# First-mixer phases of six runs instead of seven, with heads' pairs 0 and 3, 1 and 2 together

## The chip, the cores and the metric

The kernel runs on one core of a Trainium2 chip. The metric is device time in microseconds (us) of one execution; lower is better.

## The reference

Two layers over 1024 tokens of width 1024, all in float32. Of each layer only what surrounds the change matters here:

```python
h = rms_norm(x, g_mix)
qa, ka, va, qb, kb, vb, gate_logits = split(h @ w_in)
y_a = chunk_band_relbias_attention(qa, ka, va, rel_table) @ w_branch_a   # mixer A
y_b = sliding_window_sink_gqa(rope(qb), rope(kb), vb, sinks) @ w_branch_b  # mixer B
g_a, g_b = split(sigmoid(gate_logits + b_gate))
x = x + (g_a * y_a + g_b * y_b) @ w_out
x = x + (silu(g_part) * u_part) @ w_down      # of rms_norm(x) @ w_gate_up
```

Mixer A has 8 heads of 64. A 64-token chunk sees itself and the 8 chunks before it (576 keys) with a bias by relative distance. Mixer B has 8 query heads and 2 key heads, with rotary positions, a window of two chunks and a sink per head.

## The kernel before

Features lie on the 128 partitions, tokens on the free axis. The attention of a layer is 128 units in 4 groups of 32. The first 16 units of a group are its phase of mixer A: 8 blocks of 128 queries ("pairs" p = 0 to 7, for each of two heads e = 0, 1; unit u is e = u % 2 of pair u % 16 // 2). The last 16 are its phase of mixer B. Pair p of mixer A has min(p + 1, 5) blocks of 128 keys, so 128, 256, 384, 512 and then 640 columns of scores.

Units are taken in runs. `run_start` and `run_end` give a run's first and last unit. Before, a phase A has seven runs: pairs 0 and 1 together, then pairs 2 to 7 alone. A phase B has two runs of 8 units. Every engine walks a loop over the unit number s, written by hand, and all ordering between engines is by semaphores.

TensorE (PE), at the start of a run: `scores` of this run; `weigh` (probabilities times values) of the run two before; `turn_run`, the 128x128 transposes of the probabilities of the run before, into PSUM banks 5 and 1 (`t_ps`) and, where a pair has five blocks, the fifth block of both heads into half of bank 7 (`last_ps`); sometimes `turn_inverse`, one transpose of eight units' 1/sum; sometimes `turn_values`, which transposes 512 tokens of values into bank 7; and then the fill: `fill_rate(s)` steps of the product of h with the gate weights (`gate_step`, lines L1395, L1399 and L1400, three 128x512 matmuls a step). Eight steps make one half tile of gate logits in bank 0, which VectorE takes away in `scale_logit` before the next half tile may open there:

```python
if k == 0: ...
    pe.wait_ge(logit_ready, L * GATE_HALVES + i)      # gate_step, first step of half tile i
```

`FILL_A` and `FILL_B` say how many steps each run has. Before, each half tile of gates ends with the last step of some run.

VectorE (DVE), unit by unit: `row_max` (bias, row minimum of the negated scores, PSUM to the buffer of probabilities; it waits until the scores of its whole run are made), at the second unit of a run `take_inverse` and `take_heads` (outputs from PSUM to `x_sb`), reciprocals, `scale_logit` at the end of a run, and three rotary operations for each 512 columns of q of mixer B: `turn_half` at units c and c + 1 and `add_half` at c + 2, where c is 4 and 9 of a phase A of groups 1 to 3. `scores` of a run waits until `row_max` has read all of the run before (`scores_free`).

ScalarE (ACT): at the first unit of a run `soften` (exp) of that unit, then `take_turned` (transposed probabilities from PSUM to `probs_t`: two copies of up to 512 columns and one of 256 for fifth blocks) and `take_values`; then `soften` of the run's other units.

There are four buffers of probabilities. Outputs of mixer A lie in bank 6, those of mixer B in banks 4 and 6 in turn. GpSimd (POOL) splits gate weights and scales finished heads by 1/sum, SyncE (SP) issues the loads and stores, those of 1/sum through DRAM too.

Of the kernel before, what the change touches and what calls it, by code (L numbers as in the profile page):

```python
# [33 lines left out]
P = 128  # L34
# [175 lines left out]

def unit(u):

    g, r = divmod(u, UNITS_PER_GROUP)
    return "AB"[r // PHASE], g, r % 2, r % PHASE // 2


def run_start(u):
    return u & (~7 if unit(u)[0] == "B" else ~3 if u % PHASE < 4 else ~1)


def run_end(u):
    return u | (7 if unit(u)[0] == "B" else 3 if u % PHASE < 4 else 1)


FILL_A = ((8, 0, 4, 4, 2, 2, 2, 2),) + ((2, 0, 3, 2, 1, 1, 1, 0),) * (GROUPS - 1)
# [79 lines left out]
def quarters_at(s, afters):  # L305
    return [2 * eight + j for j, after in enumerate(afters) for eight in inverses_at(s, after)]
# [20 lines left out]
def turned_through(u):  # L327

    runs = {run_start(v): 3 if wide(v) else 2 for v in range(u + 1)}
    return sum(runs.values())  # L330
# [6 lines left out]
def last_wide(u):  # L337
    return max((v for v in range(u + 1) if wide(v)), default=None)
# [10 lines left out]
B_EIGHTS = EIGHTS // 2  # L349
SAVED_AFTER, SPREAD_AFTER, SCALED_AFTER = 3, (5, 6), (7, 9)  # L350
# [107 lines left out]
def build(nc, x_t, w_lin, w_gu, w_dn_a, w_dn_b, gains, gate_bias, rel, sink_in, rope_in, consts_in, out_t):  # L458
    ctx = ExitStack()
    with ctx:  # L460
# [127 lines left out]
        def s_ps(u, cols):  # L588
# [4 lines left out]
            if p == 1:  # L593
                return bank(2 + e)[:, P:P + cols]
            if cols <= HALF:
                return bank(2 + e)[:, 0:cols]
# [71 lines left out]
        def scale(engine, L, quarter):  # L668
# [5 lines left out]
            if mixer == "A":  # L674
                x = x_sb[:, g, p * P:(p + 2) * P]
                return engine.tensor_tensor(x, x, rows[:, :], ALU.mult)
# [4 lines left out]
        def turned_to(u):  # L681
            if unit(u)[0] == "A":
                return probs_t[:, u % 2, P if u % PHASE in (2, 3) else 0:]
            return probs_t[:, u % EIGHT // 4, u % 4 * P:(u % 4 + 1) * P]
# [7 lines left out]
        def soft(u):  # L692

            r = u % PHASE
            if unit(u)[0] == "B":
                first = (r // 4 + r // EIGHT) * P
                return probs[(r + 2) % NPROBS][:, first:first + P]
            if r < 4:
                return probs[r % 2][:, r // 2 * P:3 * P]
            return probs[(r + 2) % NPROBS][:, :]  # L700

        def soft_last(u):

            first = u // PHASE * PHASE
            if unit(u)[0] == "B":
                return first - NPROBS + u % NPROBS
            return first - EIGHT - 1 if u - first < 6 else u - NPROBS
# [681 lines left out]
        def _(pe):  # L1389
# [131 lines left out]
            def scores(L, u):  # L1521
# [3 lines left out]
                if mixer == "A":  # L1525
                    if u % PHASE in (0, PHASE // 2):
                        pe.wait_ge(keys_loaded[p // 4], 32 * (L * GROUPS + g + 1))
                    _, cols = score_columns("A", g, p)
                    k0 = (p + 1) * P - cols
                    if u % PHASE == 0:  # L1530
                        for pair in range(2):
                            for e in range(2):
                                rows = slice(e * HD, (e + 1) * HD)
                                width = (pair + 1) * P
                                pe.matmul(s_ps(u + 2 * pair + e, width), qa[g % 2][rows, pair * P:(pair + 1) * P], ka[g % 2][rows, 0:width],
                                          start=True, stop=True).then_inc(scores_done, 1)
                        return
                    pieces = ((0, 0, cols), (1, 0, cols)) if cols <= HALF else ((0, HALF, cols), (1, P, cols), (0, 0, HALF), (1, 0, P))
                    for n, (e, c, d) in enumerate(pieces):
# [3 lines left out]
                        mm = pe.matmul(s_ps(u + e, cols)[:, c:d], qa[g % 2][rows, p * P:(p + 1) * P], ka[g % 2][rows, k0 + c:k0 + d],  # L1543
                                       start=True, stop=True)
                        if n != 1 or cols <= HALF:
# [12 lines left out]
            def turn_run(L, last):  # L1558
# [18 lines left out]
                for e in range(2):  # L1577
                    for u in range(first + e, last + 1, 2):
                        at_col = P if u - first > 1 else 0
                        pe.wait_ge(softened, softened_through(L, u))  # L1580
                        for j in range(min(key_blocks(mixer, unit(u)[3]), A_BLOCKS - 1)):
                            mm = pe.transpose(t_ps[e][:, at_col + j * P:at_col + (j + 1) * P], soft(u)[:, j * P:(j + 1) * P], ident[:, :])  # L1582
                    mm.then_inc(turned, 1)
                if wide(last):
                    pe.wait_ge(v_ready, L * VALUES + values_before(last + 1))
                    for u in (first, last):
                        mm = pe.transpose(last_ps[:, (u - first) * P:(u - first + 1) * P], soft(u)[:, HALF:A_COLS], ident[:, :])
                    mm.then_inc(turned, 1)

            def weigh(L, u):  # L1590
# [17 lines left out]
                taken = L * HEAD_PAIRS + (u // 2 - (1 if p == 1 else 0) if mixer == "A" else run_start(u) // 2 - (2 if p % 4 < 2 else 0))  # L1608
# [1788 lines left out]
```

## Time and profile before

| | |
|---|---|
| median of 3 runs | 2589.5 us (2589.29 to 2591.73) |
| profiled execution, its own time | 2588.69 us |
| span of its profile | 2586.9 us |
| TensorE busy | 2557.4 us, 99% |
| VectorE, ScalarE, GpSimd busy | 1823.0, 1038.8, 286.4 us |

The profile was taken of one execution. Its own time is 1.8 us over the span of its instructions and 0.8 us under the median of the three runs. A matmul's end is modelled, so its row reads longer than the distance to the next matmul's start; the distances between starts say how fast TensorE moves. The matmuls on float32 heads (scores, weighing, transposes) show two rows each, those of the fills one.

### The profile page before, as it was taken

The page shows a single profiled execution, that of the slowest core. Times are in us where ns is not written, and L with a number is a line of the kernel's source. Part 1 is how long each engine was busy: PE and PEld are TensorE (multiplying, and loading weights), DVE is VectorE, ACT ScalarE, POOL GpSimd, SP SyncE. Part 2 cuts the span into 40 slices and gives each one's busy share as a digit, 9 for nine tenths or more (in the row PEclk, how much of TensorE's full clock was granted, in tenths as well). Part 3 has the DMA queues.
Part 4 walks back from the last instruction along what each step waited for, and adds up shares of the span by engine and source line. Part 5 has one row for each costly group of instructions (what it writes and reads, how often), then busy time and mean ns, then how long its engine had stood idle before and what let it go on. Part 6 is the DMA issues. An engine that isn't in the chain of part 4 may idle for free. (4 is left out here: it accounts for less than half of the span.)

```text
span 2586.9 us, 35453 instructions
## 1 busy us (share of the span) xinstructions
PE 2557.4 (99%) x12822; PEld 2095.1 (81%) x12822; DVE 1823.0 (70%) x3321; ACT 1038.8 (40%) x2035; POOL 286.4 (11%) x442
## 2 busy tenths in 40 slices
PE   8999999999999999999999999999999999999998
PEld 6888777888888888888778887778888888888886
DVE  8766555644888777768996665555459777776687
ACT  6222466522533333344542225664235333333444
POOL 0000232344000000000000002224430000000000
PEclk9999999999999999999999999999999999999999
DMA  4323543453133233395423345425422233225843
GB/s 149 130 102 114 176 140 118 135 178 115 60 116 109 90 107 122 99 280 162 151 102 117 111 136 160 145 84 179 151 106 92 88 106 118 91 97 169 260 117 126
DMA packets 200332, 336.92 MB, mean 130 GB/s; under 512 B 18672, under 2 KB 79968, under 8 KB 200160
## 3 DMA queue, kind: packets, MB, share of 16 engines
q1 hardware_dynamic: 191936, 311.47, 36.5%
q10 hardware_dynamic: 8224, 23.20, 2.6%
q8 instruction: 103, 1.69, 0.3%
q14 instruction: 69, 0.57, 0.1%
HBM read 240.76 MB, written 92.92 MB: 129 GB/s over the span
## 5 line engine op out<-in xcount | busy, mean ns | idle before, releaser
L1407 PE MATMUL ps<-op_hi,up_hi 128*128 128x512 f32 x1232 | 479.9, 389 | 2.5 <-DVE third_sum L2996 2.5
L1409 PE MATMUL ps<-op_hi,up_lo 128*128 128x512 f32 x1232 | 479.3, 389 | 0.0
L1408 PE MATMUL ps<-op_lo,up_hi 128*128 128x512 f32 x1232 | 479.3, 389 | 0.0
L1407 PE MATMUL ps<-in_hi,up_hi 128*128 128x512 f32 x728 | 285.0, 392 | 2.6 <-DVE up_lo L2491 2.1
L1408 PE MATMUL ps<-in_lo,up_hi 128*128 128x512 f32 x728 | 283.7, 390 | 0.0
L1409 PE MATMUL ps<-in_hi,up_lo 128*128 128x512 f32 x728 | 283.7, 390 | 0.0
L1407 PEld LDWEIGHTS ps<-op_hi,up_hi 128*128 128x128 f32 x1232 | 231.3, 188 | 51.0 <-issue 3.3
L1409 PEld LDWEIGHTS ps<-op_hi,up_lo 128*128 128x128 f32 x1232 | 231.3, 188 | 48.2
L1408 PEld LDWEIGHTS ps<-op_lo,up_hi 128*128 128x128 f32 x1232 | 231.3, 188 | 47.8
L2091 ACT ACTIVATE up_hi<-up_raw 128x512 fp32r<-128x512 f32 x252 | 158.1, 630 | 278.5 <-PE ps L1409 271.6
L1360 POOL CAST w_hi<-w_raw 128x256 fp32r<-128x256 f32 x184 | 81.5, 485 | 1468.0 <-DMA w_raw<-w_lin 1209.9
L1407 PE MATMUL ps<-act_hi,dn_hi 128*128 128x512 f32 x616 | 240.5, 390 | 1.2 <-DVE dn_lo L3171 1.2
L1408 PE MATMUL ps<-act_lo,dn_hi 128*128 128x512 f32 x616 | 239.7, 389 | 0.0
L1409 PE MATMUL ps<-act_hi,dn_lo 128*128 128x512 f32 x616 | 239.7, 389 | 0.0
L1944 ACT ACTIVATE probs<-probs,neg_max 128x128 f32<-128x128 f32 (+5 forms) x256 | 138.5, 545 | 145.8 <-DVE neg_max L2788 144.9
L1841 ACT ACTIVATE up_hi<-w_quarter 128x512 fp32r<-128x512 f32 x156 | 96.7, 628 | 193.8 <-PE ps L1409 182.8
L2963 DVE TENSOR_TENSOR up_lo<-up_raw,up_hi 128x512 fp32r<-128x512 f32 x252 | 172.7, 687 | 0.0
L2118 ACT ACTIVATE act_hi<-act_raw 128x512 fp32r<-128x512 f32 x154 | 97.0, 630 | 176.7 <-DMA act_raw<-ff_saved 173.5
L3169 DVE TENSOR_TENSOR act_lo<-act_raw,act_hi 128x512 fp32r<-128x512 f32 x154 | 106.3, 690 | 82.6 <-ACT act_hi L2118 81.8
L1407 PEld LDWEIGHTS ps<-in_hi,up_hi 128*128 128x128 f32 x728 | 137.0, 188 | 32.0 <-DVE up_lo L2491 3.3
L1365 POOL TENSOR_TENSOR w_lo<-w_raw,w_hi 128x256 fp32r<-128x256 f32 x192 | 160.6, 866 | 0.0
L1409 PEld LDWEIGHTS ps<-in_hi,up_lo 128*128 128x128 f32 x728 | 136.9, 188 | 28.4
(255 smaller groups left out, 4758.1 us busy)
## 6 DMA issues: line engine op xcount, KB each, us to landing
up_raw<-w_gu SPq DMA_DIRECT2D x42, 1024.0 KB, 5.1
act_raw<-ff_saved SPq DMA_DIRECT2D x154, 256.0 KB, 2.8
w_quarter<-w_lin SPq DMA_DIRECT2D x52, 512.0 KB, 4.5
w_raw<-w_lin SPq DMA_DIRECT2D x48, 512.0 KB, 4.2
ff_saved<-ff_block SPq DMA_DIRECT2D x88, 256.0 KB, 2.0
ff_saved<-ff_mix SPq DMA_DIRECT2D x66, 256.0 KB, 2.0
gated<-gates_saved SPq DMA_DIRECT2D x32, 512.0 KB, 4.2
dn<-w_dn_a SPq DMA_DIRECT2D x48, 256.0 KB, 4.0
```

Source lines behind the costliest of these rows:

```text
L1360: pool.tensor_copy(w_hi[slot][:, k, :], w_raw[raw][:, k, :]).then_inc(hi_made, 1)
L1365: op = pool.tensor_tensor(w_lo[slot][:, k, :], w_raw[raw][:, k, :], w_hi[slot][:, k, :], ALU.subtract)
L1407: pe.matmul(out, w1, x1, start=first, stop=False, skip_group_check=True)
L1408: pe.matmul(out, w1, x0, start=False, stop=False, skip_group_check=True)
L1409: return pe.matmul(out, w0, x1, start=False, stop=last, skip_group_check=True)
L1841: act.activation(up_hi[s % PRODUCTS][:, :, :], in_weight(q, i), ACT.Copy).then_inc(in_raised, 1)
L1944: act.activation(buf[:, c0:c1], buf[:, c0:c1], ACT.Exp, bias=neg_max[:, stat_of(u)], scale=-1.0, accum_out=row_sum[:, stat_of(u)]).then_in ...
L2091: act.activation(up_hi[s % PRODUCTS][:, :, :], up_src(q, i), ACT.Copy).then_inc(up_raised, 1)
L2118: act.activation(act_hi[r][:, :], act_raw[r][:, :], ACT.Copy).then_inc(act_raised, 1)
L2963: dve.tensor_tensor(up_lo[s % PRODUCTS][:, :, :], up_src(q, i), up_hi[s % PRODUCTS][:, :, :], ALU.subtract).then_inc(up_split, 1)
L3169: dve.tensor_tensor(act_lo[r][:, :], act_raw[r][:, :], act_hi[r][:, :], ALU.subtract)
```

## The change

It changes the order of mixer A's pairs to 0, 3, 1, 2, 4, 5, 6, 7 (`A_ORDER`), and the phase becomes six runs: pairs 0 and 3, pairs 1 and 2, and pairs 4 to 7 alone. The two runs of four units have five blocks for each head, like a single pair of 640 columns. All runs of mixer A now put their last block of keys into `last_ps`, and wait as those of five blocks did. The fills of a phase A become (8, 6, 4, 2, 2, 2) steps in the first group (before 8, 4, 4, 2, 2, 2, 2), and (3, 3, 1, 1, 1, 1) in the others (before 2, 3, 2, 1, 1, 1, 0). All outputs of a run lie in bank 6, of mixer B too except in the last phase, and VectorE waits for all outputs of a run before it copies the first. The transposes of 1/sum are moved (`INVERSE_LATER`). The four buffers of probabilities become two sets, taken by runs in turn, so that `row_max` waits for the transposes of the run two before. In the last phase the scaling of probabilities is two operations of 512 columns instead of four of 256.

```diff
+A_ORDER = (0, 3, 1, 2, 4, 5, 6, 7)
 def unit(u):
     g, r = divmod(u, UNITS_PER_GROUP)
-    return "AB"[r // PHASE], g, r % 2, r % PHASE // 2
+    p = r % PHASE // 2
+    return ("A", g, r % 2, A_ORDER[p]) if r < PHASE else ("B", g, r % 2, p)
 def run_start(u):
-    return u & (~7 if unit(u)[0] == "B" else ~3 if u % PHASE < 4 else ~1)
+    return u & (~7 if unit(u)[0] == "B" else ~3 if u % PHASE < PHASE // 2 else ~1)
...
-FILL_A = ((8, 0, 4, 4, 2, 2, 2, 2),) + ((2, 0, 3, 2, 1, 1, 1, 0),) * (GROUPS - 1)
+FILL_A = ((8, 0, 6, 0, 4, 2, 2, 2),) + ((3, 0, 3, 0, 1, 1, 1, 1),) * (GROUPS - 1)
...
 def inverse_at(eight):
     weighed = weighed_at(EIGHT * eight + EIGHT - 1)
-    return weighed + (4 if weighed % UNITS_PER_GROUP == 2 else 0)
+    return weighed if weighed == HELD else weighed + INVERSE_LATER[eight % len(INVERSE_LATER)]
...
-def last_wide(u):
-    return max((v for v in range(u + 1) if wide(v)), default=None)
+def last_full(u):
+    return max((v for v in range(u + 1) if unit(v)[0] == "A"), default=None)
+def block_place(p):
+    return A_BLOCKS - 1 - p if p < 2 else 0
+INVERSE_LATER = (2, 0, 8, 6)
...
         def o_ps(u):
-            mixer, _, _, p = unit(u)
-            if mixer == "A":
-                return bank(6)[:, P if p == 1 else 0:2 * P if p == 1 else P]
+            if u < LAST_UNIT - EIGHT:
+                place = (u - run_start(u)) // 2
+                return bank(6)[:, place * P:(place + 1) * P]
...
         def soft_last(u):
...
+            return run_start(run_start(u) - 1) - 1 if run_start(u) > 0 else -1
...
             def turn_values(L, s, c):
-                if last_wide(run_start(s) - 1) is not None:
-                    pe.wait_ge(turned_ready, L * TURNS + turned_through(last_wide(run_start(s) - 1)))
+                if last_full(run_start(s) - 1) is not None:
+                    pe.wait_ge(turned_ready, L * TURNS + turned_through(last_full(run_start(s) - 1)))
...
             def scores(L, u):
-                    if u % PHASE == 0:
-                        for pair in range(2):
-                            for e in range(2):
+                    if u % PHASE < EIGHT:
+                        for n, (other, e) in enumerate(((0, 0), (2, 1), (2, 0), (0, 1))):
...
             def turn_run(L, last):
-                if wide(last):
-                    pe.wait_ge(v_ready, L * VALUES + values_before(last + 1))
-                    for u in (first, last):
+                pe.wait_ge(v_ready, L * VALUES + values_before(last + 1))
+                final = key_blocks(mixer, unit(first)[3]) - 1
+                for e in range(2):
...
             def take_turned(L, last):
-                    act.activation(probs_t[:, e, 0:cols], t_ps[e][:, 0:cols], ACT.Copy).then_inc(turned_ready, 1)
-                if wide(last):
-                    act.wait_ge(turned, made + 3)
+                    act.activation(probs_t[:, e, 0:HALF], t_ps[e], ACT.Copy).then_inc(turned_ready, 1)
+                act.wait_ge(turned, made + 3)
...
             def take_heads(L, u):
-                dve.wait_ge(head_done, n + (2 if u // 2 % 2 == 0 and (mixer == "B" or p == 0) else 1))
+                if u < LAST_UNIT - EIGHT:
+                    dve.wait_ge(head_done, L * HEAD_PAIRS + run_end(u) // 2 + 1)
```

Three places show how instructions move. The first is TensorE, layer 0, group 1, the fill of the phase's first run (pairs 0 and 1 before, 0 and 3 after). `stage` holds values to be transposed, `w_hi_228` and `w_hi_229` are the gate weights of two tiles. Before:

```order
L1518 MATMUL ps<-ident,stage_100 128x128 x3
L1395 MATMUL ps<-in_hi_50,w_hi_228 128x512
L1399 MATMUL ps<-in_lo_57,w_hi_228 128x512
L1400 MATMUL ps<-in_hi_50,w_lo_230 128x512
L1395 MATMUL ps<-in_hi_50,w_hi_228 128x512
L1399 MATMUL ps<-in_lo_57,w_hi_228 128x512
L1400 MATMUL ps<-in_hi_50,w_lo_230 128x512
L1543 MATMUL ps<-ka_88,qa_90 128x384 [waits scores_free]
```

and after:

```order
L1524 MATMUL ps<-ident,stage_100 128x128 x3
L1401 MATMUL ps<-in_hi_50,w_hi_228 128x512
L1405 MATMUL ps<-in_lo_57,w_hi_228 128x512
L1406 MATMUL ps<-in_hi_50,w_lo_230 128x512
L1401 MATMUL ps<-in_hi_50,w_hi_228 128x512
L1405 MATMUL ps<-in_lo_57,w_hi_228 128x512
L1406 MATMUL ps<-in_hi_50,w_lo_230 128x512
L1401 MATMUL ps<-in_hi_56,w_hi_229 128x512 [waits logit_ready,tile_ready]
L1405 MATMUL ps<-in_lo_63,w_hi_229 128x512
L1406 MATMUL ps<-in_hi_56,w_lo_231 128x512
L1541 MATMUL ps<-ka_88,qa_90 128x256 [waits scores_free]
```

The third step of the run opens the next half tile of gates right behind the last step of the one before; before, the opening step stands in the next run, behind its scores, weighing and transposes. The same happens in every phase A: in the first group in the run of pair 4, whose four steps are two and two.

The second place is TensorE, layer 0, group 0, the transposes of the first run and the values behind them. Before:

```order
L1582 MATMUL ps<-ident,probs_105 128x128 [waits softened,logit_ready]
L1582 MATMUL ps<-ident,probs_105 128x128 [waits softened]
L1582 MATMUL ps<-ident,probs_105 128x128
L1582 MATMUL ps<-ident,probs_106 128x128 [waits softened] x2
L1582 MATMUL ps<-ident,probs_106 128x128
L1518 MATMUL ps<-ident,stage_100 128x128 [waits v_ready,stage_loaded1]
```

and after:

```order
L1590 MATMUL ps<-ident,probs_105 128x128 [waits softened,logit_ready]
L1590 MATMUL ps<-ident,probs_105 128x128 x3
L1590 MATMUL ps<-ident,probs_106 128x128 [waits softened]
L1590 MATMUL ps<-ident,probs_106 128x128 x3
L1595 MATMUL ps<-ident,probs_105 128x128 [waits v_ready]
L1595 MATMUL ps<-ident,probs_106 128x128
L1524 MATMUL ps<-ident,stage_100 128x128 [waits v_ready,stage_loaded1,turned_ready]
```

The values' transposes now wait for `turned_ready` too, the copies by ScalarE of what was transposed just ahead of them. It is the same at the third run of the first group.

The third place is VectorE, layer 0, group 1, behind the first `row_max` of the phase's second run (`ISA` with `probs` is `row_max`, the `ISA` behind it ends it). Before:

```order
L2754 TENSOR_TENSOR stage_101<-stage_101,rope 128x512 [waits stage_loaded2,rope_loaded]
L2788 ISA probs_108,neg_max<-ps,rel_sb 128x384 [waits turned,scores_done]
L2788 ISA neg_max 128x1
L2826 COPY inverse_turned<-ps 8x128 [waits inverse_saved,inverse_turned_done]
L2838 COPY x_sb<-ps 128x2x64 [waits head_done] x4
L2757 TENSOR_TENSOR swapped<-swapped,rope 128x512 [waits swap_loaded]
L2788 ISA probs_105,neg_max<-ps,rel_sb 128x512 [waits turned,scores_done]
L2788 ISA neg_max 128x1
L2768 TENSOR_TENSOR qb_93<-stage_101,swapped 128x8x64 [waits rope_step]
L2788 ISA probs_106,neg_max<-ps,rel_sb 128x512 [waits turned,scores_done]
L2788 ISA neg_max 128x1
```

and after:

```order
L2759 TENSOR_TENSOR stage_101<-stage_101,rope 128x512 [waits stage_loaded2,rope_loaded]
L2793 ISA probs_108,neg_max<-ps,rel_sb 128x256 [waits turned,scores_done]
L2793 ISA neg_max 128x1
L2846 COPY x_sb<-ps 128x2x64 [waits head_done] x4
L2762 TENSOR_TENSOR swapped<-swapped,rope 128x512 [waits swap_loaded]
L2793 ISA probs_107,neg_max<-ps,rel_sb 128x384 [waits turned,scores_done]
L2793 ISA neg_max 128x1
L2773 TENSOR_TENSOR qb_93<-stage_101,swapped 128x8x64 [waits rope_step]
L2793 ISA probs_108,neg_max<-ps,rel_sb 128x384 [waits turned,scores_done]
L2793 ISA neg_max 128x1
```

Before, these rows belong to two runs, one of 384 and one of 512 columns. After, all of it is one run (pairs 1 and 2), with one more `row_max` of 256 columns ahead of it, and the copy of 1/sum has moved out of it.

## Rows read from the trace of the kernel before

**Rows 1.** The page: span.

```profile
span 2586.9 us, 35453 instructions
```

**Rows 2.** Windows: time, each engine's busy time (instructions), TensorE's granted clock, DMA.

```profile
279.00:500.00 221.00, 220.94 (x1711) 172.77 (x1710) 129.08 (x436) 132.54 (x380) 64.93 (x97) 1.00 0.42 132
...
1300.00:1320.00 20.00, 17.87 (x79) 14.48 (x78) 19.48 (x31) 10.41 (x19) 0.00 (x0) 1.00 0.13 47
```

**Rows 3.** Timeline, PE: scores that open runs, layer 0, group 2: start, us.

```profile
381.89 0.93 PE L1535 MATMUL ps<-ka,qa 64*128 64x128 f32 x8
...
386.81 0.92 PE L1543 MATMUL ps<-ka,qa 64*128 64x384 f32 x4
...
403.88 1.35 PE L1543 MATMUL ps<-ka,qa 64*128 64x128 f32 x8
...
408.34 1.35 PE L1543 MATMUL ps<-ka,qa 64*128 64x128 f32 x8
...
412.10 1.16 PE L1555 MATMUL ps<-kb,qb 64*128 64x64 f32 x16
```

**Rows 4.** Timeline, PE, inside the first and the sixth of these runs.

```profile
382.74 0.44 PE L1619 MATMUL ps<-probs_t,vb_odd 128*64 128x128 f32 x4
...
383.77 1.09 PE L1573 MATMUL ps<-ident,probs 128*128 128x128 f32 x8
384.70 0.27 PE L1626 MATMUL ps<-ident,inverse 128*8 128x128 f32 x1
384.81 0.60 PE L1518 MATMUL ps<-ident,stage 128*128 128x128 f32 x4
...
385.70 0.40 PE L1400 MATMUL ps<-keep_hi,w_lo 128*128 128x512 f32 x1
...
386.40 0.40 PE L1400 MATMUL ps<-keep_hi,w_lo 128*128 128x512 f32 x1
...
405.16 1.31 PE L1619 MATMUL ps<-probs_t,va 128*64 128x128 f32 x20
406.40 1.09 PE L1582 MATMUL ps<-ident,probs 128*128 128x128 f32 x8
```

**Rows 5.** Timeline, DVE, the first three of these runs.

```profile
386.34 0.41 DVE L2788 CUSTOM_DVE_ANT_0 probs<-ps,rel_sb 128x256 f32<-128x256 f32 x1
...
386.83 0.69 DVE L2851 TENSOR_TENSOR logit<-ps,rstd 128x512 f32<-128x512 f32 x1
387.94 0.56 DVE L2788 CUSTOM_DVE_ANT_0 probs<-ps,rel_sb 128x384 f32<-128x384 f32 x1 [0.42 <-PE ps L1543]
...
388.43 0.69 DVE L2754 TENSOR_TENSOR stage<-stage,rope 128x512 f32<-128x512 f32 x1
...
389.91 0.86 DVE L2838 COPY x_sb<-ps 128x128 f32<-128x128 f32 x4
390.70 0.67 DVE L2757 TENSOR_TENSOR swapped<-swapped,rope 128x512 f32<-128x512 f32 x1
...
393.61 0.95 DVE L2768 TENSOR_TENSOR qb<-stage,swapped 128x512 f32<-128x512 f32 x1
```

**Rows 6.** Timeline, later in layer 0: PE held by DVE for a bank.

```profile
716.35 0.69 DVE L2996 TENSOR_TENSOR third_sum<-ps,first_sum 128x512 f32<-128x512 f32 x1
...
717.19 0.47 PE L1407 MATMUL ps<-op_hi,up_hi 128*128 128x512 f32 x1 [1.26 <-DVE third_sum L2996]
```

**Rows 7.** Timeline, ACT and PE: `take_turned` behind the transposes of a run.

```profile
287.38 0.87 PE L1582 MATMUL ps<-ident,probs 128*128 128x128 f32 x6
...
288.88 0.85 ACT L1972 ACTIVATE probs_t<-ps 128x384 f32<-128x384 f32 x2
...
368.24 0.48 PE L1395 MATMUL ps<-in_hi,w_hi 128*128 128x512 f32 x1
...
367.86 1.09 ACT L1972 ACTIVATE probs_t<-ps 128x512 f32<-128x512 f32 x2 [0.77 <-PE ps L1582]
368.83 0.39 ACT L1975 ACTIVATE probs_t<-ps 128x256 f32<-128x256 f32 x1
```

More of the change, by code:

```diff
@@ L305, in quarters_at @@
 def quarters_at(s, afters):
-    return [2 * eight + j for j, after in enumerate(afters) for eight in inverses_at(s, after)]
+    return sorted(2 * eight + j for j, after in enumerate(afters) for eight in inverses_at(s, after))
 def inverses_before(u):
@@ L327, in turned_through @@
 def turned_through(u):
-    runs = {run_start(v): 3 if wide(v) else 2 for v in range(u + 1)}
+    runs = {run_start(v): 3 if unit(v)[0] == "A" else 2 for v in range(u + 1)}
     return sum(runs.values())
@@ L592, in s_ps @@
                 return bank(2 + e)[:, p % 4 * P:p % 4 * P + cols]
[L593 to L596, printed above, removed]
+            if p < 2:
+                return bank(3)[:, 2 * P * e:2 * P * e + cols]
+            if p < 4:
+                return bank(2 + 2 * e)[:, 0:cols]
             start = 5 * HALF - A_COLS if e else 2 * HALF
@@ L681, in turned_to @@
         def turned_to(u):
-            if unit(u)[0] == "A":
-                return probs_t[:, u % 2, P if u % PHASE in (2, 3) else 0:]
+            mixer, _, e, p = unit(u)
+            if mixer == "A":
+                return probs_t[:, e, block_place(p) * P:]
             return probs_t[:, u % EIGHT // 4, u % 4 * P:(u % 4 + 1) * P]
@@ L692, in soft @@
         def soft(u):
[L694 to L700, printed above, removed]
+            mixer, _, e, p = unit(u)
+            if mixer == "B":
+                return probs[2 * (p // 4) + e][:, p % 4 * P:(p % 4 + 1) * P]
+            later = u % PHASE // 4 == 1 if u % PHASE < EIGHT else u % 4 > 1
+            return probs[2 * later + e][:, block_place(p) * P:A_COLS]
         def soft_last(u):
[L704 to L707, printed above, removed]
+            return run_start(run_start(u) - 1) - 1 if run_start(u) > 0 else -1
         def gain_at(n, k):
@@ L1578, in turn_run @@
                     for u in range(first + e, last + 1, 2):
-                        at_col = P if u - first > 1 else 0
+                        pair = unit(u)[3]
                         pe.wait_ge(softened, softened_through(L, u))
-                        for j in range(min(key_blocks(mixer, unit(u)[3]), A_BLOCKS - 1)):
-                            mm = pe.transpose(t_ps[e][:, at_col + j * P:at_col + (j + 1) * P], soft(u)[:, j * P:(j + 1) * P], ident[:, :])
+                        for j in range(min(key_blocks(mixer, pair), A_BLOCKS - 1 - block_place(pair))):
+                            place = block_place(pair) + j
+                            mm = pe.transpose(t_ps[e][:, place * P:(place + 1) * P], soft(u)[:, j * P:(j + 1) * P], ident[:, :])
                     mm.then_inc(turned, 1)
-                if wide(last):
-                    pe.wait_ge(v_ready, L * VALUES + values_before(last + 1))
-                    for u in (first, last):
-                        mm = pe.transpose(last_ps[:, (u - first) * P:(u - first + 1) * P], soft(u)[:, HALF:A_COLS], ident[:, :])
-                    mm.then_inc(turned, 1)
+                pe.wait_ge(v_ready, L * VALUES + values_before(last + 1))
+                final = key_blocks(mixer, unit(first)[3]) - 1
+                for e in range(2):
+                    mm = pe.transpose(last_ps[:, e * P:(e + 1) * P], soft(first + e)[:, final * P:(final + 1) * P], ident[:, :])
+                mm.then_inc(turned, 1)
             def weigh(L, u):
@@ L1607, in weigh @@
                 pe.wait_ge(turned_ready, L * TURNS + turned_through(u) - (1 if wide(u) or mixer == "B" and u % EIGHT < 4 else 0))
-                taken = L * HEAD_PAIRS + (u // 2 - (1 if p == 1 else 0) if mixer == "A" else run_start(u) // 2 - (2 if p % 4 < 2 else 0))
+                taken = L * HEAD_PAIRS + run_start(u) // 2
                 if taken > 0:
@@ L1966, in take_turned @@
                     return
-                cols = 3 * P if last - first == 3 else min(key_blocks(mixer, p) * P, HALF)
                 for e in range(2):
@@ L2813, in scale_last @@
                 dve.wait_ge(inverse_step, L * (EIGHTS + 1) + EIGHTS)
-                own = inverse[:, stats_of(EIGHTS - 1)].rearrange("p (r i o) -> p i r o", i=4, o=1)
-                for i in range(4):
-                    both = probs[(i + 2) % NPROBS][:, 3 * P:5 * P].rearrange("p (r n) -> p r n", r=2)
-                    op = dve.tensor_tensor(both, own[:, i, :, :].to_broadcast([P, 2, P]), both, ALU.mult)
+                own = inverse[:, stats_of(EIGHTS - 1)].rearrange("p (r e o) -> p e r o", e=2, o=1)
+                for e in range(2):
+                    both = probs[2 + e][:, 0:HALF].rearrange("p (r n) -> p r n", n=P)
+                    op = dve.tensor_tensor(both, own[:, e, :, :].to_broadcast([P, HALF // P, P]), both, ALU.mult)
                 op.then_inc(inverse_step, 1)
```

35 lines of the change are left out of this document (20 added, 15 removed).

## The prediction

> **What bounds the kernel now.** I read the page first. TensorE is busy nearly all of the span [rows 1], but a matmul's modelled end hides short gaps, so I went by windows and by distances between starts. In the window over the first layer's attention TensorE is busy for 220.94 of 221.00 us, with a granted clock of 1.00 (2.4 GHz), while VectorE has 129 us and ScalarE 133 us of work [rows 2]. So inside attention TensorE waits for nobody: the time there is the sum of what it issues, and the other engines' slack is free. A change in these phases can only act in two ways. It can change what TensorE's own stream costs, or it can use up slack until TensorE stands.
>
> The timeline of TensorE is like clockwork. In layer 0, group 2, the seven runs of phase A start at 381.89 and mixer B starts at 412.10 [rows 3], so the phase takes 30.21. A full run (640 columns, one step of fill) takes 4.46 (403.88 to 408.34). Inside it scores take 1.28 (403.88 to 405.16) and weighing 1.24 [rows 3, 4]. The first run of the phase takes 4.92, with scores of 0.85 and 1.03 of weighing mixer B's outputs [rows 3, 4].
>
> **What the regrouping saves.** The number of matmuls, their sizes and the steps of fill stay the same; only the fixed costs of a run are paid six times rather than seven. I build the new phase from rows of the old.
> - Run of pairs 0 and 3: 4.92, plus 0.43 because its scores are 640 columns a head (1.28 against 0.85), plus one more step of fill, 0.70 (385.70 to 386.40 [rows 4]), less 0.11 for the transpose of 1/sum that moves out (384.70 to 384.81). That is 5.94.
> - Run of pairs 1 and 2: a full run with two more steps, 4.46 + 1.40, less 0.21 since it weighs mixer B's outputs (1.03 against 1.24). That is 5.65.
> - Runs of pairs 4, 5 and 6: 4.46 + 0.11, as the moved transposes of 1/sum stand there. Pair 7: 4.46 with its one step.
>
> The sum is 5.94 + 5.65 + 3 x 4.57 + 4.46 = 29.76, against 30.21: 0.45 saved. The first group has longer fills, but loses one run in the same way; I take 0.45 there too. Eight phases (4 groups, 2 layers) save **3.6 us**. The order of the two-pair scores is that of a 640-column pair (both heads, small piece first), so I see no reason for another price; bounds are 0 (only moved) and 0.8 a phase.
>
> **What it adds, first: the gate bank.** Eight steps fill bank 0, and then `scale_logit` must empty it. Before, the last of eight steps closed a run, so VectorE had a whole run's scores, weighing and transposes as cover. With fills of 3, or of 4 after a 6, the ninth step follows the eighth at once: the order shows its wait for `logit_ready` in the middle of the fill. In the trace the last matmul of a half tile starts at 386.40 [rows 4], `scale_logit` starts at 386.83 and takes 0.69 [rows 5], so it ends at 387.52. For the way back I use a place where TensorE really stood for VectorE: `third_sum` ends at 717.04 and the matmul starts at 717.19 [rows 6], 0.15 later. So the next step starts 1.27 after the last matmul of the eighth, where matmuls of a fill are otherwise 0.23 apart. TensorE stands 1.04. VectorE is there in time: in the first run its four `row_max` (two of 128, two of 512 columns) and four copies are over before the second step ends. Eight places (every phase A) cost **8.3 us**; bounds 0.8 and 1.5 each. The bank can't be read while it is written: the Trainium skill (PSUM — Partial Sum Buffer, "PSUM bank collisions raise a hardware error") has no two engines on one bank at a time, which fits the 0.04 between the modelled end of the last matmul (386.80) and the start of `scale_logit`, and so doesn't allow the overlap that would hide it.
>
> **Second: the values' bank.** All runs of mixer A now use `last_ps`, half of the bank of the values. In the first group, `turn_values` at the second and third run thus waits for ScalarE's three copies of the run just transposed; before, no wait stood there. At the third run the case is that of a full run: two copies start at 367.86, the third starts at 368.83 and ends at 369.22, where TensorE went on with its next work at 368.24 [rows 7]. With 0.15 for the way back it would go on at 369.37: 1.13 lost. At the second run nothing is weighed ahead, and ScalarE comes late from its first exp: before, its copy there started 1.50 after the transposes (287.38, 288.88 [rows 7]). With 256 columns instead of 384 in that `row_max` and exp, some 0.13 shorter each, 1.24. Then 0.97 to the third copy, 0.39 for it and 0.15 back make 2.75, where TensorE's own transposes take about 1.09 [rows 4]: 1.66 lost. Together 2.8 a layer, **5.6 us**; bounds 1.5 and 3.5 a layer. In the other groups values are turned behind mixer B's transposes, and the wait is long met.
>
> **Third: VectorE in the run of pairs 1 and 2.** In groups 1 to 3 three rotary operations now fall into one run, between its four `row_max`. From starts [rows 5]: `row_max` of 256 columns 0.34 (0.41 long, and the next starts 0.07 before its end), rotary 0.62, `row_max` 0.34, four copies 0.79 (389.91 to 390.70), rotary 0.60, `row_max` of 384 0.49 (387.94 to 388.43), `add_half` 0.88, `row_max` 0.49: 4.55 in all. VectorE starts 1.56 into the run: scores 1.28, and 0.28 more as from 386.81 to 387.94 with scores of 0.85 [rows 3, 5]. From the last `row_max` to TensorE's next scores is 0.13 more than its step (386.34, 386.81 [rows 3, 5]). So the next scores may start at 1.56 + 4.55 + 0.13 = 6.24, where TensorE is ready at 5.65: 0.59 lost at six places, **3.5 us**; bounds 0 and 1.0 each. This had cover before since two runs (4.8 and 4.1 us) shared the work. What is queued behind `add_half` is the last `row_max`, and for that TensorE waits.
>
> **What costs nothing.** Outputs in one bank: TensorE must find the heads of all earlier runs taken, but VectorE copies them inside the run before, ahead of its last `row_max`. Probability sets in turn: they free VectorE from a wait that TensorE did not feel. The moved 1/sum: three saves now come in consecutive runs of 4.57, and a save had 4.9 before; POOL's scaling comes behind a gate tile's split, and SP may stand for it, but bias, keys and gate tiles are wanted runs later. If one of these is late, the cost is a few us a layer (last rival). The two scalings of 512 columns at the end lie under gate steps.
>
> **Sum.** -3.6 + 8.3 + 5.6 + 3.5 = +13.8 us, against the profiled execution's own time of 2588.7: 2602.5. The median of the runs shown lies 0.8 above that execution, less than I can tell; I predict **2602.5 us**, 0.5% slower.
>
> **Rivals.**
> - *Only the waits that the order writes between neighbours cost (gate bank, values' bank); VectorE's chain finds slack.* That is -3.6 + 13.9 = +10.3, or with the low bounds of both (0.8 and 1.5 a layer) +5.8: 2594.5 to 2599. For it: my chain adds eight steps, and 0.08 less in each closes the gap. Against: the trace's steps repeat to 0.02. Chance 0.17 for 2594.7 to 2599.
> - *The waits are covered and only fixed costs count: faster.* Its one mechanism is that TensorE's queue hides the turnaround at the gate bank, as at the ends of runs, where `scale_logit` costs it nothing. It would give 2588.7 - 3.6 = 2585. It decides if all stalls together are under 3.6 us, that is under 0.45 a phase, and from there it is faster; against it stands that `scale_logit` alone takes 0.69, while the order leaves nothing between the two steps. Chance 0.04 for all below 2594.7 that is not within the next.
> - *The change hardly tells,* because the stalls are near my low bounds and the saving near 0.8 a phase: -6.4 + 6.4 + 3.0 = +3, 2592. Chance 0.06.
> - *Late 1/sum.* If VectorE waits for a save's landing at two transposes a group, or a gate tile comes late, some 2 us at each of six phases are added: +26, 2615. Against: saves have 4.6 us. Chance 0.08 above 2609.
> - *The clock falls after the new stalls.* One of 1.66 us or less would have to do what an idle stretch of 2.1 us in 1300 to 1320 did not: there TensorE is busy 17.87 of 20.00, and the granted clock stays 1.00 [rows 2]. If each of 18 stalls cost 1 us more, 2620. The Trainium skill (TensorE: Matmul & The Clock Gate, "A second HAM failure mode: psum-queue depth-cycling") tells of short idle times between groups of matmuls that bring the clock down again and again; by that rule this rival would be the likely one, and the row speaks against it. Chance 0.02.
>
> **How the numbers follow.** The forecast (2599 to 2609) has 0.63. The first rival's 0.17 lies right under it; the others have 0.20. The range from 2596 to 2609 holds the forecast and most of the first rival, about 0.78. Faster and slower by over 0.2% (5.2 us, about what a measurement of this kernel can tell from no change) are under 2584.3 and over 2594.7. Slower: 0.63 + 0.17 + 0.08 + 0.02 = 0.90. The other two rivals share the rest: same 0.08, as even the covered case at 2585 lies within 0.2%, faster 0.02.
>
> **What would show each step.** In the changed kernel's timeline: a phase A of groups 1 to 3 takes 29.8 plus 1.04 plus 0.59, about 31.4 instead of 30.2; TensorE idles about 0.9 before the first matmul of a half tile once in each phase, released by `scale_logit`; it idles before the values' transposes at the second and third run of each layer, released by `probs_t`; and the scores behind the run of pairs 1 and 2 start late, released by `row_max`. Wrong would be: starts of fill steps still 0.23 apart across a half tile, TensorE waiting for tiles or 1/sum, or a granted clock below 1.00 within attention.

## The result and the profile after

The changed kernel takes **2611.45 us** (median of 5 runs, 2609.19 to 2614.75). The kernel before takes 2589.29 us on the same chip (5 runs). The ratio is 1.0086, with a 95% interval of 1.0071 to 1.0100. It is slower, as forecast, but by 22.2 us and not by 13.8, and it lies 2.5 us above the range.

The profiled execution's own time is 2614.75 us, against 2588.69. In the windows view (time, busy time of PE, PEld, DVE, ACT and POOL with instructions, granted clock, DMA share, GB/s) the first row covers the first layer's attention:

```profile
280.00:501.00 221.00, 209.02 (x1652) 166.17 (x1651) 116.69 (x422) 125.48 (x371) 55.61 (x84) 0.99 0.39 122
```

In [rows 2] TensorE was busy for 220.94 of 221.00 us. Now 12 us are missing, and 59 matmuls fewer fit into the window. The view of waits for TensorE, same kernel, whole span (us in total, times, longest), names who held it:

```profile
PE ps L1627 <- DVE x_sb L2846: 7.7, 4, 2.5
PE ps L1401 <- DVE logit L2859: 6.6, 8, 0.9
PE ps L1524 <- ACT probs_t L1981: 4.3, 4, 1.3
PE ps L1550 <- DVE neg_max L2793: 3.4, 6, 0.8
```

None of the four stands in the same view of the kernel before. The last three are the stalls of the forecast: the gate bank (eight times), the values' bank (four times), VectorE's chain in the run of pairs 1 and 2 (six times). The first, 7.7 us, is the one that I had priced at nothing. (The idle time of a row begins at the modelled end of the matmul before, so what a stall costs is read below from starts and from lengths of runs, and comes out larger.)

**The three that were forecast.** The timeline of TensorE (start, duration, and in brackets the idle time before it with its releaser), layer 0, group 1, last two steps of the first run's fill and on to the next scores:

```profile
343.65 0.40 PE L1406 MATMUL ps<-in_hi,w_lo 128*128 128x512 f32 x1
344.92 0.47 PE L1401 MATMUL ps<-in_hi,w_hi 128*128 128x512 f32 x1 [0.88 <-DVE logit L2859]
...
345.79 1.45 PE L1541 MATMUL ps<-ka,qa 64*128 64x256 f32 x8
...
352.39 0.92 PE L1550 MATMUL ps<-ka,qa 64*128 64x128 f32 x4 [0.81 <-DVE neg_max L2793]
```

From 343.65 to 344.92 are 1.27, as forecast (a start without a wait comes 0.23 later), and the matmul behind the stall takes 0.31 to the next start and not 0.23. The run of pairs 1 and 2 lasts from 345.79 to 352.39, 6.60. VectorE inside it:

```profile
347.41 0.42 DVE L2793 CUSTOM_DVE_ANT_0 probs<-ps,rel_sb 128x256 f32<-128x256 f32 x1 [2.63 <-PE ps L1541]
...
347.76 1.12 DVE L2759 TENSOR_TENSOR stage<-stage,rope 128x512 f32<-128x512 f32 x1
348.80 0.41 DVE L2793 CUSTOM_DVE_ANT_0 probs<-ps,rel_sb 128x256 f32<-128x256 f32 x1
...
351.11 0.74 DVE L2773 TENSOR_TENSOR qb<-stage,swapped 128x512 f32<-128x512 f32 x1
351.78 0.54 DVE L2793 CUSTOM_DVE_ANT_0 probs<-ps,rel_sb 128x384 f32<-128x384 f32 x1
```

From start to start, `add_half` (351.11) takes 0.67 where I had 0.88, but `turn_half` (347.76) takes 1.04 where I had 0.62. Both sizes were off, and in part they cancel. And the values, layer 0, group 0, second run:

```profile
290.29 0.38 PE L1595 MATMUL ps<-ident,probs 128*128 128x128 f32 x2
291.98 0.65 PE L1524 MATMUL ps<-ident,stage 128*128 128x128 f32 x4 [1.31 <-ACT probs_t L1981]
```

```profile
291.54 0.38 ACT L1981 ACTIVATE probs_t<-ps 128x256 f32<-128x256 f32 x1
```

ScalarE's third copy ends at 291.92 and TensorE goes on 0.06 later, not the 0.15 that I had taken.

**The one that was not.** Layer 0, group 1, the run of pair 7. TensorE stands behind its scores, before it may weigh:

```profile
366.11 1.35 PE L1550 MATMUL ps<-ka,qa 64*128 64x128 f32 x8
369.89 1.31 PE L1627 MATMUL ps<-probs_t,va 128*64 128x128 f32 x20 [2.44 <-DVE x_sb L2846]
```

It waits for `take_heads` (L2846) to free the outputs' bank. VectorE there:

```profile
360.94 0.28 DVE L2831 COPY inverse_turned<-ps 8x128 f32<-8x128 f32 x1 [0.24 <-PE ps L1634]
...
361.55 0.67 DVE L2773 TENSOR_TENSOR qb<-stage,swapped 128x512 f32<-128x512 f32 x1
...
369.31 0.28 DVE L2831 COPY inverse_turned<-ps 8x128 f32<-8x128 f32 x1 [4.64 <-DMA inverses_saved<-inverse_turned]
369.52 0.27 DVE L2846 COPY x_sb<-ps 128x128 f32<-128x128 f32 x1
```

`take_inverse` (L2831) may not write the next eight sums over the last ones until these are saved. It stands 4.64, and `take_heads` is queued behind it. Why the save was late is to be read in SP's queue:

```profile
362.24 1.73 SPq L1050 DMA_DIRECT2D swapped<-in_saved  x4
364.01 1.62 SPq L1203 DMA_DIRECT2D rope<-rope_in  x1
365.68 0.50 SPq L1220 DMA_DIRECT2D inverses_saved<-inverse_turned  x1
```

The sums were copied by 361.22. Their save was issued at 365.68, behind four loads that had waited for `add_half` and behind the load of a rotary table, and VectorE went on 3.6 after that: 8.4 from one `take_inverse` to the next, where the runs leave 4.57. The larger part of the 8.4 is the queue. The Trainium skill (DMA: Bandwidth & Descriptors, "Latency and other measured facts") gives some 2 us of fixed cost and puts most of it down to memory, whose latency grows under load. The 3.6 for 4 KB are longer than that; the DMA share was 0.47 in the window 364 to 368, and no run here shows how much of the 3.6 is memory. This run lasts 6.97 instead of 4.46 (366.11 to 373.08). The four such runs (groups 1 and 2, both layers) are 2.51, 2.53, 1.40 and 1.50 too long, 7.9 us, and one of them pays 1.46 more for the clock. The second layer loses less because the table's load takes 0.6 to issue there, where it takes 1.6 in the first: from one `take_inverse` to the next are 8.37, 8.40, 7.26 and 7.37. In all four, what TensorE loses is this path less 5.86, to 0.02. The windows of the run with the lower clock, layer 0, group 2:

```profile
416.00:420.00 4.00, 2.09 (x13) 1.22 (x11) 0.02 (x1) 1.57 (x5) 0.00 (x0) 1.00 0.56 173
420.00:424.00 4.00, 3.45 (x27) 3.15 (x28) 2.23 (x7) 0.97 (x3) 0.73 (x1) 0.57 0.21 59
```

TensorE was idle for 2.46 there, and in the 4 us behind it the mean granted clock is 0.57, so it was mostly at the lower of its two levels, 1.2 GHz; `weigh` takes 2.34 instead of 1.24.

### The profile page after: what moved, and what is told of

Read it like the earlier page. It is cut to its first block and busy times, and to the rows that moved or that the text cites. A ratio compares the mean times of both kernels' runs of the same rounds, so it can differ in the third digit from the quotient of the medians.

```text
span 2612.9 us, 35441 instructions
## 1 busy us (share of the span) xinstructions
PE 2562.1 (98%) x12822; PEld 2105.8 (81%) x12822; DVE 1819.1 (70%) x3317; ACT 1039.5 (40%) x2035; POOL 286.1 (11%) x442
## 5 line engine op out<-in xcount | busy, mean ns | idle before, releaser
L1414 PEld LDWEIGHTS ps<-in_lo,up_hi 128*128 128x128 f32 x728 | 137.9, 189 | 28.3
```

The costliest lines, as they stand in the source:

```text
L1414: pe.matmul(out, w1, x0, start=False, stop=False, skip_group_check=True)
```

## The experiments

**1. Save sooner.** One edit on the changed kernel:

```diff
-SAVED_AFTER, SPREAD_AFTER, SCALED_AFTER = 3, (5, 6), (7, 9)
+SAVED_AFTER, SPREAD_AFTER, SCALED_AFTER = 1, (5, 6), (7, 9)
```

> The changed kernel, with each save of 1/sum to DRAM issued two units sooner on SyncE's queue, and so ahead of the rotary loads that wait for add_half. Theory (queue order): the third copy of 1/sum of a phase waited 4.6 us on VectorE because the save before it stood behind loads that wait for add_half and take 3.5 us to issue; the save now goes out some 4 us sooner, VectorE's wait at that copy is under 0.5 us, TensorE's waits of 2.5, 2.5, 1.4 and 1.5 us in the run of pair 7 (groups 1 and 2) are gone: about 7.9 us less than the changed kernel's 2611.4, 2603.5. Rival (landing time): three saves in consecutive runs can't land in time wherever they are issued; the waits stay, 2611.

Measured: 2606.86 us (4 runs), ratio 1.0069 (1.0054 to 1.0084). The wait L1627 <- L2846 is gone from the view of waits, and every run of pair 7 lasts 4.46. Both layers' attention together is 14.1 us longer than before, where my sum gave 13.8. The time is 3.4 us above what I expected, though, and part of that is a new wait, which stands behind attention:

```profile
PE ps L1401 <- DVE o_lo L2895: 1.2, 6, 0.4
```

The reason shows in this line of the same kernel (number, shortest, middle and longest duration in ns):

```profile
L2895 DVE TENSOR_TENSOR o_lo<-x_sb,o_hi x16: 1209/1511/1760, 490.9 to 1785.0; 128x1024 fp32r<-128x1024 f32 x16
```

In the changed kernel without this edit, which has not that wait, it reads:

```profile
L2895 DVE TENSOR_TENSOR o_lo<-x_sb,o_hi x16: 1208/1211/1769, 495.4 to 1791.6; 128x1024 fp32r<-128x1024 f32 x16
```

So the middle one of VectorE's operations there is slower by a quarter; experiments 7 and 8 show why.

**2. Turn later.** Also on the changed kernel, instead of the first edit:

```diff
-INVERSE_LATER = (2, 0, 8, 6)
+INVERSE_LATER = (4, 0, 8, 6)
```

> The changed kernel, with the third transpose of 1/sum of a phase one run later (pair 7's run instead of pair 6's), queue order as it is. Queue order and landing time both say that the save before it has landed by then (it landed 3.2 us into pair 7's run, the copy comes 4.0 us into it): waits gone, 2603.5. If instead TensorE's waits in pair 7's run come from something else (heads in one bank), they stay: 2611.

Measured: 2605.2 us (4 runs), ratio 1.0061 (1.0046 to 1.0076). The stall is gone here too, with the save where it was. Attention is 14.7 us over before (the time is 1.7 above what I expected). Either the earlier save or the wider distance between turns is enough, so it is the distance from save to turn that counts.

**3. Fills cut at whole banks.**

```diff
-FILL_A = ((8, 0, 6, 0, 4, 2, 2, 2),) + ((3, 0, 3, 0, 1, 1, 1, 1),) * (GROUPS - 1)
+FILL_A = ((8, 0, 8, 0, 2, 2, 2, 2),) + ((2, 0, 4, 0, 1, 1, 1, 1),) * (GROUPS - 1)
```

> The changed kernel, with fills of (8, 8, 2, 2, 2, 2) and (2, 4, 1, 1, 1, 1) steps, so that each half tile of gates again ends with a run. Theory (gate bank): the eight waits of 1.04 us for scale_logit go, 8.4 us; and the run of pairs 1 and 2 becomes 0.7 us longer, which covers VectorE's chain, 3.3 us more: 2611.4 - 11.7 = 2599.7, with no wait of TensorE for logit or neg_max in attention. Rival (the stall only moves): what TensorE doesn't wait for the gate bank it waits for elsewhere, and under 4 us come back: above 2607.

Measured: 2604.59 us (4 runs), ratio 1.0064 (1.0047 to 1.0081). The eight waits for `logit` are gone, and so are the six for `neg_max`: with four steps the run of pairs 1 and 2 lasts 6.40 in groups 1 to 3 and hides the chain (6.57 once). Attention is 10.6 us shorter than in the changed kernel, where I expected 11.7, as the wait for the save grew; the time is 4.9 above what I expected. TensorE's waits in this kernel, and VectorE at the same place as above:

```profile
PE ps L1627 <- DVE x_sb L2846: 9.4, 4, 3.8
```

```profile
366.94 0.28 DVE L2831 COPY inverse_turned<-ps 8x128 f32<-8x128 f32 x1 [5.99 <-DMA inverses_saved<-inverse_turned]
```

The four runs of pair 7 are 11.3 us too long against 9.4 in the changed kernel, in both with the lower clock in one of them; without the clock that is 9.7 against 7.9. (The expectation of experiment 7 sets the 7.9 without the clock beside the 11.3 with it.) The runs that the save has to itself are not shorter: between the second and the third turn lie 4.57 in both kernels. It is the save's own path that grew, from 8.4 to 9.7 at the place shown. With the fills moved, a gate tile's load (`w_raw`, 512 KB) now stands ahead of the save too:

```profile
358.51 2.02 SPq L1050 DMA_DIRECT2D swapped<-in_saved  x4
360.57 0.42 SPq L996 DMA_DIRECT2D w_raw<-w_lin  x1
361.04 1.18 SPq L1203 DMA_DIRECT2D rope<-rope_in  x1
362.26 0.50 SPq L1220 DMA_DIRECT2D inverses_saved<-inverse_turned  x1
```

VectorE goes on 4.7 after this issue. It is so in group 1 of both layers (path 9.73 and 8.57). In group 2, where no gate tile's load stands there, the path is 7.83 and 6.98, shorter than in the changed kernel. At all four places TensorE again loses the path less 5.86.

**4. The moved sums alone,** on the kernel before (seven runs, its fills and banks), with the quarters to be spread put in order:

```diff
-    return weighed + (4 if weighed % UNITS_PER_GROUP == 2 else 0)
+    return weighed if weighed == HELD else weighed + INVERSE_LATER[eight % 4]
...
-    return [2 * eight + j for j, after in enumerate(afters) for eight in inverses_at(s, after)]
+    return sorted(2 * eight + j for j, after in enumerate(afters) for eight in inverses_at(s, after))
...
+INVERSE_LATER = (2, 0, 8, 6)
```

> The kernel before, with the moved transposes of 1/sum alone (INVERSE_LATER and the sorted list of quarters). Theory (queue order): the three transposes stand in consecutive runs here too, the save of the second stands behind the same loads, so VectorE waits 4 to 5 us at the third in groups 1 and 2 and TensorE 1 to 2.5 us: 2589.3 + 4 to 9 = 2593 to 2598. Rival: the wait needs the six-run phase or the one bank of outputs; then this is 2589 to 2590.

Measured: 2603.3 us (4 runs), ratio 1.0054 (1.0037 to 1.0071). That is 14 us, much more than either theory had. Its attention is 13.4 us longer than before. The last runs of phase A in groups 1 and 2 are 13.7 longer (10.38, 7.72, 5.82 and 4.86 instead of the 3.76 of [rows 3]), the others together 0.3 shorter. TensorE's waits, and windows over two of these runs:

```profile
PE ps L1620 <- DVE x_sb L2839: 9.7, 4, 4.4
```

```profile
361.00:375.00 14.00, 9.63 (x83) 7.84 (x83) 3.88 (x14) 5.13 (x13) 2.19 (x3) 0.76 0.40 129
413.00:424.00 11.00, 8.71 (x76) 7.01 (x72) 3.87 (x13) 5.66 (x13) 0.73 (x1) 0.84 0.39 118
```

In group 1 of the first layer a gate tile's load stands ahead of the save, as in experiment 3, and the path from turn to turn is 10.3. The four paths (10.30, 8.23, 7.91 and 6.95) less 5.86 each make 9.95 us; the other 3.8 are the clock, which is at the lower level behind both stalls of the first layer. Moving the 1/sum is by itself as dear as all that I had forecast for the change.

**5. Values later** (three of the first group's operands, in steps of s):

```diff
-CONV_START = (1, 3, 6, 4, 10, 6, 8, 20)
+CONV_START = (1, 3, 6, 5, 10, 9, 11, 20)
```

> The changed kernel with the values of the first group turned one, three and three steps later (their starts 4, 6, 8 become 5, 9, 11), so that their bank is free when they come. If the 1.47 and 0.98 us by which the values' pieces in the second and third run of group 0 last longer than in the kernel before (5.1 us in two layers with the small rest) are a wait for that bank, 5.1 us go: about 2606.3 us. Rival: the wait only moves to the next copy out of that bank, and the time stays at 2610 to 2612 us. The wait for the 1/sum save in groups 1 and 2 is not touched and should still be there (7 to 9 us).

Measured: 2607.58 us (4 runs), ratio 1.0067 (1.0054 to 1.0081). The four waits for `probs_t` are gone, and attention is 5.5 us shorter than in the changed kernel, where I expected 5.1. The other waits stay, 6.9 us for `take_heads` among them. The time is 1.3 above what I expected.

**6. Rotary later,** so that SP issues its loads behind the save:

```diff
-                    for r in (24 - UNITS_PER_GROUP, 0, 4, 9))
+                    for r in (24 - UNITS_PER_GROUP, 0, 6, 12))
...
-ROPE_TIMES = (12, 45, 77)
+ROPE_TIMES = (12, 47, 79)
```

> The changed kernel with the rotary work of a group two to three steps later and its table loads at steps 47 and 79 instead of 45 and 77, so that SP issues the 1/sum save ahead of them instead of behind them. If the save lands late because it stands behind four swapped loads and the table load in SP's queue, the wait in pair 7's run (7.9 us with its clock dip of 1.4) goes and VectorE's chain in the run of pairs 1 and 2 loses its late rotary too (up to 3.5): about 2600 us. Rival: the save is late by its own two steps and landing of 3 us, whatever stands ahead of it; then 2607 to 2611 us.

Measured: 2598.97 us (5 runs), ratio 1.0031 (1.0019 to 1.0043). SP's queue in it, layer 0, group 1:

```profile
354.25 1.71 SPq L1050 DMA_DIRECT2D swapped<-in_saved  x4
356.01 4.33 SPq L1220 DMA_DIRECT2D inverses_saved<-inverse_turned  x2
```

The second of these two saves goes out at 360.1, 0.3 after the start of its copy (359.77), where it had been 4.7; nothing stands between turn and save. Neither `SAVED_AFTER` nor the turns were touched. So the wait was made by what stood ahead of the save in the queue, and not by its own steps. Group 3 of the changed kernel says the same: no swapped loads and no table stand there, and both saves go out as soon as they can, with no stall behind them:

```profile
459.92 4.84 SPq L1220 DMA_DIRECT2D inverses_saved<-inverse_turned  x2
```

The run of pairs 1 and 2 is down to 5.72, so this edit also measures the chain: the six runs of the changed kernel are 6.60, 6.01, 6.41, 6.61, 6.01 and 6.54, together 3.9 over 5.72 each. What is left is what the other stalls should leave: attention is 10.2 us over before.

**7 and 8. All stalls taken out.** Experiment 7 has edits 1, 3 and 5 together, experiment 8 has 2, 3 and 5.

> Three edits on the changed kernel at once: the 1/sum saved one step after it is turned instead of three, the gate fills cut at whole banks, and the values of group 0 later. If the four stalls (gate bank 8.4, values 5.1, VectorE's chain in the run of pairs 1 and 2 3.5, the wait for the save 7.9 us with 1.4 of a clock dip) are all there is against the six-run phase, attention falls to that of the kernel before less 3.6 to 3.9 us, and the time is about 2585.5 us, faster than the kernel before. Rival: what one edit frees comes back as a longer wait for the save (with the fills alone cut at banks it grew from 7.9 to 11.3 us); then 2590 us or more.

Measured: 2589.4 us (11 runs) beside 2589.54 us of the kernel before (22 runs), ratio 0.9998 (0.9989 to 1.0007). The attention came out nearly as expected (3.5 us shorter than before), and the longer wait for the save of the rival didn't come; but the time is 3.9 above what I expected, and no different from the kernel before.

> As the run with three edits, but instead of an earlier save the 1/sum of the held run's successor is turned two runs later (4 instead of 2), which keeps two runs between each pair of turns. If only the distance between a save and the next turn matters, the time is the same as with the earlier save, about 2585.5 us, within 2 us of it. Rival: the later turn pushes the spread into the next run's work and POOL's multiply comes late; then 2588 us or more.

Measured: **2585.82 us** (11 runs), ratio 0.9983 (0.9975 to 0.9992). This is the best of all, 3.7 us under the kernel before, and the whole interval lies below 1. The window of [rows 2] for it:

```profile
279.00:500.00 221.00, 221.00 (x1720) 178.17 (x1720) 124.95 (x434) 133.95 (x382) 64.44 (x99) 1.00 0.42 133
```

TensorE waits for nobody in it. Each layer's attention, from the first scores to those of its last run, is 184.26 and 184.27 against 186.13 before: 0.47 for each of eight phases. In experiment 7 attention is as short (184.28 and 184.51). The two times are not within the 2 us of each other that I expected, since experiment 7 loses behind attention: there the earlier saves end so that POOL splits gate weights while VectorE makes the low parts of the outputs. VectorE and POOL in experiment 7, then VectorE in experiment 8:

```profile
479.68 11.20 DVE L2895 TENSOR_TENSOR o_lo<-x_sb,o_hi 128x1024 fp32r<-128x1024 f32 x8 [1.13 <-ACT o_hi L2017]
```

```profile
478.09 3.82 POOL L1371 TENSOR_TENSOR w_lo<-w_raw,w_hi 128x256 fp32r<-128x256 f32 x4
481.86 3.40 POOL L690 TENSOR_TENSOR x_sb<-x_sb,inverse_rows 128x256 f32<-128x256 f32 x2
```

```profile
478.58 9.72 DVE L2895 TENSOR_TENSOR o_lo<-x_sb,o_hi 128x1024 fp32r<-128x1024 f32 x8 [1.13 <-ACT o_hi L2017]
```

The eight operations take 11.20 and not 9.72, and TensorE, which eats them as they come, falls back by 1.4 us in the first layer and 1.75 in the second, by the starts of the first `o_hi` matmul and of the tenth in both kernels. That is 3.2 of the 3.6 us between the two kernels' medians. It fits that experiment 1, with the same edit, ends above experiment 2 though its attention is no longer.

## Why the forecast was too low

Taken in its own order, with what the runs showed:

- *What the regrouping saves, 0.45 a phase:* right. Experiment 8, with no stall left, shows 0.47, 3.7 us in all. Building a run of the new kernel out of rows of the old one works, as the starts repeat to 0.02. Two small misses cancel: the scores of pairs 1 and 2 (256 columns first) take 1.38 and not 1.28, and the run of pairs 0 and 3 comes to 5.86 and not 5.94 (5.16 in experiment 8, with a fill step of 0.70 less).
- *The gate bank, 1.04 each, 8.3 us:* right. From start to start it measured 1.04 at the place shown and 0.95 to 1.05 at the others. By the lengths of the runs beside those of experiment 3 it is 1.04 to 1.11, 8.7 in all, as the first matmul behind each stall is slower by 0.08. It goes with the fills (experiment 3).
- *The values' bank, 5.6 us:* right in mechanism, sized 0.5 too high. From the lengths of the first group's runs in experiment 5 it is 5.1 (2.56 a layer); the rest of the 5.5 there is in other groups. The 0.15 for the way back had come from a wait on VectorE; ScalarE released TensorE after 0.06.
- *VectorE's chain, 0.59 each, 3.5 us:* right as a mechanism, and 3.9 by experiment 6, but that the total fits is in part luck. In group 2, where each rotary operation takes 0.6 to the next start, a run loses 0.29, half of my 0.59, as `add_half` is cheaper than I had it. In group 1 it loses 0.88, since `turn_half` takes 1.12 there, and in group 3 0.69 and 0.82.
- *What costs nothing:* this is the step that failed, in the words "The moved 1/sum: three saves now come in consecutive runs of 4.57, and a save had 4.9 before". That sentence compares a distance between turns with a distance in the kernel before, and neither is the save's own path. Of a moved step every issue counts, and the save stands in SP's queue behind swapped loads that wait for `add_half`, and behind the table's load. From one turn to the next it needs 8.4 in the first layer and 7.3 in the second, not 4.57. Experiments 1, 2 and 6 each take the stall away by another means (save ahead, turn behind, loads behind), and experiment 4 makes it alone. It is 7.9 us, and 1.5 for the clock behind the longest.
- *The rival "late 1/sum"* named the mechanism and the engine, VectorE waiting for a save's landing, and got 0.08 since I allowed 4.6 to a save without reading when SP would issue it. Its price was too high: not six phases but four, as in group 3 no loads stand ahead of the save.
- *The rival "the clock falls"* came in small: behind one stall of 2.46, for 1.5 us. I had priced the stalls that I knew, none over 1.7, and behind those it did not fall. But the row that I set against this rival was luck. The idle stretch of 2.1 in it is a wait for `up_lo`, in code that no edit here touches. It is there in all ten profiled executions (2.08 to 2.14), and in the 4 us from its end the granted clock is 1.00 in five of them and 0.57 to 0.70 in the other five. Here are the kernel before and experiment 7:

```profile
1310.00:1314.00 4.00, 4.00 (x18) 3.29 (x19) 4.00 (x8) 2.44 (x5) 0.00 (x0) 1.00 0.00 0
1310.00:1314.00 4.00, 4.00 (x12) 3.13 (x12) 3.90 (x7) 2.31 (x5) 0.00 (x0) 0.57 0.00 0
```

The sum of what was measured in attention is -3.7 + 8.7 + 5.1 + 3.9 + 7.9 + 1.5 = 23.4, and the two profiles differ there by 23.4 (13.45 in the first layer, 9.98 in the second). The 2.6 us that the profiled executions differ by beyond that are mostly two more stretches at the lower clock (0.91 from 30 to 50 us, 0.83 from 1320 to 1330) and 0.4 more of waiting for the first input, at places that the change doesn't touch; without them and the 1.5 the sum is 21.9, near the 22.2 between the medians.

## What to carry to other kernels

Where a step moves in one engine's program, follow its data to the end through each queue that it passes: when will the DMA be issued, what stands ahead of it there, and who waits for that. A distance between two issues is not the time that a save has. An edit that mends one stall can also change what stands in that queue, so look at the trace again after each: with the fills mended the wait for the save grew from 7.9 us to 9.7, since a gate tile's load had moved in front of it. At the sixteen places of the changed kernel and of experiments 3, 4 and 5, TensorE lost the path from turn to turn less 5.86, within 0.02, and the clock on top where it fell. So such a loss can be worked out, once the path is read rather than guessed.

## What the hardware showed that I had not expected

- A stall of 2.46 us on TensorE (group 2) is followed by a granted clock of 0.57 over 4 us, but that of 2.44 in group 1 by 1.00, and so are those of 1.31 and 0.88. In experiment 3 one of 2.65 is not followed by the lower level, in experiments 4 and 5 ones of 2.29 and 2.27 are. With the wait for `up_lo`, where the same idle time in the same code has it in five of ten executions, this says that length alone did not decide it; what did is open. Experiment 3 spread most (2601.9 to 2611.9), with a mean clock of 0.994 in its slowest execution and 0.997 in its fastest.
- VectorE and POOL slow each other down where VectorE's operation has two inputs from SBUF. `turn_half` takes 1.12 in group 1, beside POOL's split of gate weights, and 0.69 in group 2, where POOL does nothing:

```profile
346.92 3.25 POOL L1371 TENSOR_TENSOR w_lo<-w_raw,w_hi 128x256 fp32r<-128x256 f32 x4
```

```profile
398.99 0.69 DVE L2759 TENSOR_TENSOR stage<-stage,rope 128x512 f32<-128x512 f32 x1
```

  The low parts of the outputs take 1.40 instead of 1.21 each. `row_max`, with one input from PSUM and one from SBUF, stays at 0.41 beside the same split (348.80). The Trainium skill (SBUF — State Buffer, "Terms") has VectorE and GpSimd share a pair of ports under an exclusive lock, held for a full instruction, with the loser fully blocked. The rows agree that they disturb each other. `turn_half` lost 0.43 beside instructions of 0.8, which is less than one of them. In experiment 6 it is POOL that loses: a `turn_half` at 349.30 keeps its 0.69, and the scaling on POOL beside it takes 1.19 and not 0.73.
- SP needs 1.7 to 2.3 us to issue four loads of 64 KB, and 0.6 to 1.7 for one table. A queue is itself a resource that a 4 KB save has to wait for. From its issue to VectorE's going on this save took 3.3 to 4.1 at twelve places, and 4.0 to 5.0 at the four where a gate tile's load of 512 KB had been issued just before it; that the load slows the save is likely, but no run here tries it alone.
